# Latent attention in a two-block transformer kernel: the order of copies on ScalarE, of projections on TensorE, and of the result's transposes

## What is computed

```python
def mla_mixer(h, pos, w_in, q_norm, w_qb, kv_norm, w_kvb, w_out):
    ...
    q = (rms_norm(q_lat, q_norm) @ w_qb).reshape(B, S, H, QK_NOPE + QK_ROPE)   # H = 16, 64 + 32
    ...
    kv = (rms_norm(kv_lat, kv_norm) @ w_kvb).reshape(B, S, H, QK_NOPE + V_HEAD)
    ...
    def attend(args):
        blk, qn, qr = args                                   # blocks of 128 queries
        s = (jnp.einsum('bqhd,bkhd->bhqk', qn, k_nope)
             + jnp.einsum('bqhr,bkr->bhqk', qr, k_rope)).astype(jnp.float32) * scale
        ...
        s = jnp.where(causal, s, MASK_VALUE)
        p = jax.nn.softmax(s, axis=-1).astype(v.dtype)
        return jnp.einsum('bhqk,bkhd->bqhd', p, v)
    ...
    return o @ w_out
```

## Time and profile before

| what | us |
|---|---|
| median of three runs | 3055.1 |
| lowest and highest run | 3048.0, 3055.36 |
| the profiled execution: its own time | 3062.72 |
| the profiled execution: span from first to last instruction | 3061.4 |
| TensorE busy, of the span | 2843.2 (93%) |
| VectorE, ScalarE, GpSimd busy | 1717.6, 1235.7, 248.7 |

### The profile page before, as it was taken

How to read it: one execution, slowest core, us unless ns; L and a number is a source line. 1 busy time by engine, 2 the same in 40 slices (tenths; PEclk the granted TensorE clock), 3 DMA queues, 4 the chain that set the end, 5 groups by cost and what they waited for, 6 DMA issues and landing times. The chain is left out here.

```text
span 3061.4 us, 36282 instructions
## 1 busy us (share of the span) xinstructions
PE 2843.2 (93%) x14489; PEld 2326.9 (76%) x14489; DVE 1717.6 (56%) x2889; ACT 1235.7 (40%) x2128; POOL 248.7 (8%) x224
## 2 busy tenths in 40 slices
PE   5988899999997989989999997999999999899998
PEld 4766687877886879778877775788788766678886
DVE  6666455444873857444468886543425386654344
ACT  2455432223433343333467775432223345432222
POOL 0000000000002543010000001112100002200000
PEclk8889999999999999989999999999999999999999
DMA  5222234332222111064579995211231203412321
GB/s 221 76 109 102 83 144 172 137 128 93 96 110 90 56 42 56 1 222 140 186 269 367 342 362 208 76 66 42 101 113 46 83 31 129 150 69 81 116 83 66
DMA packets 72096, 387.66 MB, mean 127 GB/s; under 512 B 8234, under 2 KB 9934, under 8 KB 36174
## 3 DMA queue, kind: packets, MB, share of 16 engines
q1 hardware_dynamic: 58512, 349.20, 31.4%
q10 hardware_dynamic: 10382, 26.07, 2.4%
q0 software_dynamic: 3024, 9.98, 0.9%
HBM read 368.43 MB, written 22.03 MB: 128 GB/s over the span
## 5 line engine op out<-in xcount | busy, mean ns | idle before, releaser
L343 DVE TENSOR_TENSOR wlo<-stage,whi 128x1024 fp32r<-128x1024 f32 (+3 forms) x504 | 531.5, 1095 | 356.2 <-ACT whi L355 354.8
L355 ACT ACTIVATE whi<-stage 128x1024 fp32r<-128x1024 f32 (+3 forms) x504 | 440.4, 922 | 230.8 <-PE ps L639 195.8
L639 PE MATMUL ps<-bxhi,whi 128*128 128x512 f32 x480 | 200.9, 418 | 17.1 <-DVE bxlo L343 8.4
L639 PE MATMUL ps<-whi,mxhi 128*128 128x512 f32 (+1 forms) x528 | 204.2, 387 | 9.9 <-DVE wlo L343 7.8
L639 PE MATMUL ps<-whi,mxlo 128*128 128x512 f32 (+1 forms) x528 | 197.8, 375 | 0.0
L639 PE MATMUL ps<-wlo,mxhi 128*128 128x512 f32 (+1 forms) x528 | 197.5, 374 | 0.0
L639 PE MATMUL ps<-bxhi,wlo 128*128 128x512 f32 x480 | 190.4, 397 | 0.0
L639 PE MATMUL ps<-bxlo,whi 128*128 128x512 f32 x480 | 189.9, 396 | 0.0
L343 DVE TENSOR_TENSOR wlo<-more,whi 128x1024 fp32r<-128x1024 f32 (+1 forms) x126 | 142.2, 1171 | 44.3 <-ACT whi L355 43.1
L351 DVE SCALAR_TENSOR_TENSOR part<-stage,small,part 128x256 f32<-128x256 f32 x273 | 157.9, 579 | 9.7
L639 PE MATMUL ps<-gwide 128*128 128x128 f32 x1088 | 135.8, 285 | 13.4 <-POOL gwide L343 11.5
(11 more groups left out here) (591 smaller groups left out, 6311.6 us busy)
## 6 DMA issues: line engine op xcount, KB each, us to landing
stage<-in_gu SPq DMA_DIRECT2D x92, 1024.0 KB, 5.5
stage<-in_ada SPq DMA_DIRECT2D x40, 1024.0 KB, 5.1
more<-in_gu SPq DMA_DIRECT2D x40, 1024.0 KB, 7.0
stage<-in_dn SPq DMA_DIRECT2D x26, 768.0 KB, 4.5
stage<-in_dn SPq DMA_DIRECT2D x19, 1024.0 KB, 7.1
stage<-in_gin SPq DMA_DIRECT2D x16, 1024.0 KB, 4.9
stage<-in_gt SPq DMA_DIRECT2D x16, 1024.0 KB, 5.0
more<-in_dn SPq DMA_DIRECT2D x13, 1024.0 KB, 6.7
```

Source lines behind the costliest of these rows:

```text
L343: return e.do.tensor_tensor(out, x, y, op)
L355: return e.do.activation(out, x, f, **kw)
L639: return self.p.do.matmul(out, lhsT, rhs, start=start, stop=stop, skip_group_check=True)
```

## The change

It does four things.

1. In ScalarE's step the copy of the turned tile of unit n - 3 now stands ahead of the exponential of unit n.
2. The ten triples of a group's projection are spread over six steps: two in each of steps 1 to 4, one each in steps 5 and 6. With them move `queries` (step 3 to 4, on ScalarE and VectorE), ScalarE's `keys` (step 4 to 6) and the split of wk (step 2 to 4).
3. The transposes of the result (`across`) leave the place after the loop: seven of the eight pairs go into steps 58 to 64, each between `turn` and `values`, with their split on ScalarE and VectorE at the end of the same step; the eighth goes into the output projection, after its fourth triple. Their banks are 5 and 6 in turn.
4. Both halves of piece 0 of wo are split in step 61, those of piece 1 in step 63.

```diff
--- before.py
+++ after.py
@@ -890,6 +890,14 @@
         units = self.mla_units()
         more = None
 
+        def across(m):
+            ps, vacant = self.take(("ot", m), at=5 + m % 2)
+            p.wait_ge(*vacant)
+            for i in range(4):
+                p.wait_ge(A(free(("o", 4 * (2 * m + 1) + i))))
+                z = self.tr(ps[:, i * P:(i + 1) * P], L.O[:, i, m * P:(m + 1) * P])
+            z.then_inc(*P_.up(("ot", m)))
+
         def scores(n):
             h, i = units[n]
             w, k = (i + 1) * P, h % 4
@@ -914,30 +922,26 @@
             z.then_inc(*P_.up(("o", n)))
 
         for n in range(64 + 4):
-            if n % 8 == 0 and n < 56:
-                more = self.mla_project(L, n // 8 + 1)
-            step = more if n % 8 and n < 64 else iter(())
+            if n % 8 == 0:
+                more = self.mla_project(L, n // 8 + 1) if n < 56 else iter(())
             if n < 64:
                 scores(n)
-            next(step, None)
+            if n % 8 in (1, 2, 3, 4):
+                next(more, None)
             if 3 <= n < 67:
                 turn(n - 3)
-            next(step, None)
+            if n % 8 in (1, 2, 3, 4, 5, 6):
+                next(more, None)
+            if 58 <= n < 65:
+                across(n - 58)
             if n > 3:
                 values(n - 4)
-            next(step, None)
             if n >= 8 and (n - 8) % 4 == 0 and (n - 8) // 4 < 12:
                 self.pe_ada(0, 8 + (n - 8) // 4)
         self.banks(range(7))
-        for m in range(8):
-            ps, vacant = self.take(("ot", m))
-            p.wait_ge(*vacant)
-            for i in range(4):
-                p.wait_ge(A(free(("o", 4 * (2 * m + 1) + i))))
-                z = self.tr(ps[:, i * P:(i + 1) * P], L.O[:, i, m * P:(m + 1) * P])
-            z.then_inc(*P_.up(("ot", m)))
-        for _ in self.pe_gemm("wo", "wo", range(4), L.X, lambda q: [V(("ot", "l", q))]):
-            pass
+        for k, _ in enumerate(self.pe_gemm("wo", "wo", range(4), L.X, lambda q: [V(("ot", "l", q))])):
+            if k == 3:
+                across(7)
 
     def mla_act(self, L):
         a, A, P_, V = self.a, self.A, self.P, self.V
@@ -1012,18 +1016,9 @@
         queries(0)
         self.act_ahead("wk0", 0)
         keys(0)
+        self.act_ahead("wq", 1, False)
         for n in range(64 + 4):
             g = n // 8 + 1
-            if n < 64:
-                w = (units[n][1] + 1) * P
-                c, sl = L.cols[n % 6], L.sl[n % 5]
-                a.wait_ge(V(("nm", n)))
-                act(a, sl[:, 0:w], sl[:, 0:w], ACT.Exp, bias=c[:, 5:6], scale=L.scale, accum_out=c[:, 4:5]).then_inc(*A.up(("e", n)))
-            if n % 8 == 2 and g < 8:
-                self.act_ahead("wq", g, False)
-                self.act_ahead(f"wk{g}", 0, False)
-            if n % 8 == 4 and g < 8:
-                keys(g)
             if 3 <= n < 67:
                 u = n - 3
                 w = (units[u][1] + 1) * P
@@ -1031,8 +1026,16 @@
                 if u >= 4:
                     a.wait_ge(P_(("o", u - 4)))
                 act(a, L.pt[u % 4][:, 0:w], self.bank(("t", u))[:, 0:w], ACT.Copy).then_inc(*A.up(free(("t", u))))
-            if n % 8 == 3 and g < 8:
+            if n < 64:
+                w = (units[n][1] + 1) * P
+                c, sl = L.cols[n % 6], L.sl[n % 5]
+                a.wait_ge(V(("nm", n)))
+                act(a, sl[:, 0:w], sl[:, 0:w], ACT.Exp, bias=c[:, 5:6], scale=L.scale, accum_out=c[:, 4:5]).then_inc(*A.up(("e", n)))
+            if n % 8 == 4 and g < 8:
+                self.act_ahead(f"wk{g}", 0, False)
                 queries(g)
+            if n % 8 == 6 and g < 8:
+                keys(g)
             if n > 3:
                 u = n - 4
                 h, i = units[u]
@@ -1042,10 +1045,11 @@
                 act(a, L.O[:, i, h * 64:h * 64 + 64], self.bank(("o", u))[:, 0:64], ACT.Copy, scale=L.cols[u % 6][:, 6:7]).then_inc(*A.up(free(("o", u))))
             if n % 8 == 7 and g < 7:
                 self.act_ahead("wq", g + 1, False)
-        for m in range(8):
-            if m == 0:
-                a.wait_ge(P_(("o", 63)))
-            self.act_high("ot", L.X, m, self.bank(("ot", m))[:, :], P_(("ot", m)))
+            if 58 <= n < 65:
+                self.act_high("ot", L.X, n - 58, self.bank(("ot", n - 58))[:, :], P_(("ot", n - 58)))
+            if n in (61, 63):
+                self.act_ahead("wo", 0, n == 63)
+        self.act_high("ot", L.X, 7, self.bank(("ot", 7))[:, :], P_(("ot", 7)))
         for n in range(4):
             self.act_ahead("wo", n)
             for m in (2 * n, 2 * n + 1):
@@ -1146,6 +1150,7 @@
         self.dve_ahead("wq", 0)
         queries(0)
         self.dve_ahead("wk0", 0)
+        self.dve_ahead("wq", 1, False)
         v.wait_ge(self.Dt[0]("tab"))
 
         def modulation():
@@ -1169,10 +1174,8 @@
                     *V.up(free(("s", n))))
                 v.wait_ge(V.now())
                 ts(v, c[:, 5:6], c[:, 0:1], -L.scale, None, MUL).then_inc(*V.up(("nm", n)))
-            if n % 8 == 2 and g < 8:
-                self.dve_ahead("wq", g, False)
+            if n % 8 == 4 and g < 8:
                 self.dve_ahead(f"wk{g}", 0, False)
-            if n % 8 == 3 and g < 8:
                 queries(g)
             if n > 3:
                 c = L.cols[(n - 4) % 6]
@@ -1182,12 +1185,15 @@
                 self.dve_ahead("wq", g + 1, False)
             if n > 1:
                 next(more, None)
+            if 58 <= n < 65:
+                self.dve_low("ot", L.X, n - 58, self.bank(("ot", n - 58))[:, :], P_(("ot", n - 58)), done=[free(("ot", n - 58))])
+            if n in (61, 63):
+                self.dve_ahead("wo", 0, n == 63)
         for _ in more:
             pass
         self.dve_mod(0, 4)
         self.dve_gain("n2", 0, 3, "nf0")
-        for m in range(8):
-            self.dve_low("ot", L.X, m, self.bank(("ot", m))[:, :], P_(("ot", m)), done=[free(("ot", m))])
+        self.dve_low("ot", L.X, 7, self.bank(("ot", 7))[:, :], P_(("ot", 7)), done=[free(("ot", 7))])
         for n in range(4):
             self.dve_ahead("wo", n)
             for m in (2 * n, 2 * n + 1):
```

## The result

The changed kernel takes 3068.76 us (median of 10 runs, 3066.27 to 3087.64), the kernel before 3052.66 us (10 runs, 3043.5 to 3059.17). The ratio, taken of the means, is 1.0069, 95% interval 1.0047 to 1.0091: slower, where I had forecast 3042.6 us and a range up to 3059. Seven of the ten runs lie at 3066 to 3074 us, three at 3083 to 3088 with a mean granted clock of 0.955 instead of 0.960 to 0.962. The profiled execution took 3073.73 us, with a span of 3072.4.

What follows compares the result with a forecast made beforehand. TensorE, busy 93% of the span, bounds the kernel, leaving its stalls and clock to gain. Terms -1.7 - 9.6 + 1.2 - 10.4 + 8.0 = -12.5, from 3055.1 gave 3042.6 us; range 3028 to 3059.

Steps and rivals of the forecast that it cites:

- Groups at full clock 23.0 us: Attention loop: a group of eight steps takes 23.0 us at full clock instead of 24.59.
- The walk's five stalls: TensorE stalls left in one group, found by following the engines' queues: 0.3, 0.5, 0.5, 0.4, 0.9, together 2.6 us.
- The load wait of 2.08: ScalarE's wait for the wk piece in step 2: said to go, as wk is split two steps later.
- Whatever the attention ends earlier should come through: Behind the attention: its gain reaches the total, since output projection and feed-forward are matmuls back to back with weights loaded ahead.
- a fall in every group: Rival, attention loop: the clock falls in each group, seven times 4.0 to 4.8 us; 3065.4, up to 3071 us; chance 0.07.
- The clock term, -10.4 + 8.0: Attention: three falls costing 10.4 us in the profile before are replaced by two falls at 4.0 us each.
- The number of falls: Attention: one to three stretches at 1.2 GHz, two taken for the forecast, fewer than before because stalls are shorter.
- Wrong if the clock falls five times or more: Sign set beforehand: five or more falls of the clock would show the forecast wrong.
- The tail, +1.2: Last steps to output projection: the moved transposes cost 1.2 us with the clock up, 4.0 with it down.
- the slow start of the projection (2.8): Output projection: its start at half clock, half of 5.7 us, was to come back as a gain of 2.8 us.
- The rival of the slow tail: Rival: the clock falls in step 61 and lasts into the output projection; tail 4.0, 2.8 us more, 3045.4 us; chance 0.08.
- The six groups, -9.6: Attention loop: six groups each 1.6 us shorter at full clock, 9.6 us less in all.

Runs made afterwards that it cites:

- a_waits5: The changed kernel with waits that make five instructions more in VectorE's stream, ahead of the second block's dilated attention: 3050.92 us.
- b_hold: The kernel before with three extra matmuls where TensorE idles at the start of the second block's dilated attention: 3052.11 us.
- b_waits123: The kernel before with waits that make 123 instructions more in VectorE's stream, ahead of the second block's dilated attention: 3069.28 us.
- b_tail: The kernel before with only the transposes of the result and their two copies moved into the last steps: 3087.02 us.

## Why the prediction was wrong

- *Groups at full clock 23.0 us:* right, 22.73. The walk's five stalls (0.3, 0.5, 0.5, 0.4, 0.9) came at their places and measured 0.22, 0.73, 0.30, 0.47 and 0.71, 2.43 us against 2.6. The load wait of 2.08 is gone.
- *The step that failed first: "Whatever the attention ends earlier should come through".* Only the back-to-back matmuls right behind the attention had been looked at. 1940 us later stands a stage that starts with TensorE waiting for VectorE and ScalarE, and that kept its clock with a wait of 0.58 us and lost it with one of 0.94. The change moved no instruction there, but it took five out of VectorE's stream. The slower case I had priced, a fall in every group at 4.0 to 4.8 us each, is not what made the kernel slower: falls came in nearly every group, but cost less. The loss was one fall, of 23.0 us in the profile and some 18 in the medians (3068.8 against 3050.9), in another stage. With it taken away the changed kernel is level with the one before (a_waits5, 1.0001), so the forecast gain of 12.5 us is missing all the same; the next points say where.
- *The clock term, -10.4 + 8.0, rested on one execution.* The profiled run of before had three falls in the attention and lay 10 us above the later median. The same attention code in b_hold had two, in b_waits123 one, and they reached the feed-forward at 374.1 and 369.4 us against 380.3. I had seen that the profile was 7.6 above the median and applied the difference to either all the same. The changed kernel's attention, in six profiles, reaches that point at 369.1 to 373.7 us: 0.4 to 5.0 ahead of b_hold, and between 0.2 ahead of b_waits123 and 4.3 behind it, not 11.2 ahead.
- *The number of falls* was one to three in the forecast; it was one in nearly every group (five, and one in the tail), as in the rival, but shorter: from step 28 on some 3.4 us at 1.2 GHz and 1.5 us lost in each group, where the kernel before had stretches of 13.7 us that I had priced at 3.5. "Wrong if the clock falls five times or more" has come true. That the price of the falls still came out near the 8.0 of the sum is luck: the five groups from 153.57 to 275.68 take 8.5 us more than five times 22.73, by more falls than forecast at less apiece than the 4.0.
- *The tail, +1.2:* mis-sized. From step 56 to the output projection 29.5 us against 28.2 walked, and the slow start of the projection (2.8) did not come back, since the clock was down from about 303 to 320 us. From step 56 to the feed-forward it is 83.3 us against 77.6 in b_hold: 5.7. The rival of the slow tail had the better picture with 4.0. The Trainium skill's rule (TensorE: Matmul & The Clock Gate, Part 4: PE-mode transpose), that transposes do not count as busy, gave that side; but the clock fell at the end of an idle time of 2.44 us, and no run here separates that from the transposes.
- *The six groups, -9.6:* the size holds at full clock (six times 24.59 less 22.73 is 11.2), but not the cause. I gave the spread the load wait and `mlaqh`, and the turned copy the `probt` stalls, and added them. The turned copy alone gives 19 to 20 us, more than the whole change was forecast to give; the spread beside it costs 9 to 12.

## What to carry to other kernels

Try each part of a change alone before they are put together; here the first of three gave some 20 us, and the other two beside it took them back. Take a clock term from several executions, never from one profile. Where a change loses time in a stage that it doesn't touch, compare that stage's first microseconds, waits and instruction fetches included, and test with a few idle instructions: a stage whose engines start by waiting for each other can hang on 0.35 us.

## What the runs showed of the hardware

- Once down, the clock stayed at 1.2 GHz for 47.8 us (the changed kernel) and 78.5 us (b_waits123), with TensorE shown busy 4.00 of 4.00 us in the windows, in a stage of short matmuls (64 rows, 64 columns, transposes); in b_tail the same stage had it back after 17.1 us, and the first attention after 3.4 to 17.1 us.
- Where a boundary of VectorE's instruction stream (one in about 128 instructions) lay between two dependent passes, the second came 0.35 us later (0.79 against 0.44). The profile shows this as a wait for TensorE, though TensorE's matmuls ran as in the kernels without it.
- Executions of the same attention code reached the next stage up to 11 us apart (369.4, 374.1 and 380.3 us), with one, two and three falls of the clock in it.
